# One 512-column product in place of two of 256 columns in 83 weight units of a float32 block kernel, the halves added by VectorE

## What is computed

```python
xn = rmsnorm(h, norm1_g)                      # h: (1, 256, 1024)
p = xn @ w_in                                 # 1024 x 5408: attention, RWKV, gates
# attention of 8 heads, an RWKV-7 time mix of 8 heads, both gated and projected
h = h + y @ w_out
xn = rmsnorm(h, norm2_g)
q = xn @ peer_wq                              # 16 query units of 128 columns
s = einsum('thpc,hpnc->thpn', q, peer_subkeys)
top_s, top_i = top_k(s, 16)                   # then top 16 of 256 pairs per head
gates = softmax(best_s)
h = h + sum_k(gelu(u[idx] . xn) * gates * v[idx])   # 16384 experts, 128 a head and token
return rmsnorm(h, normf_g)
```

## Time and profile before

| | us |
|---|---|
| median of 3 runs | 1074.61 (1073.79 to 1075.15) |
| the profiled execution, its own time | 1073.91 |
| its span, first to last instruction | 1072.1 |
| TensorE busy | 1063.4 (7680 products) |
| VectorE busy | 694.3 |
| ScalarE busy | 613.7 |
| GpSimd busy | 475.5 |
| mean DMA rate | 169 GB/s |

### The profile page before, as it was taken

The page is one execution under the profiler, slowest core; times in us unless marked ns, Lnnn a source line. Parts: engine busy times, 40 slices in busy tenths (PEclk is TensorE's granted clock), DMA queues, the critical chain, the costliest instruction groups (busy, mean ns, idle before and its releaser), DMA issues.

```text
span 1072.1 us, 23070 instructions
## 1 busy us (share of the span) xinstructions
PE 1063.4 (99%) x7680; PEld 985.2 (92%) x7680; DVE 694.3 (65%) x1475; ACT 613.7 (57%) x1122; POOL 475.5 (44%) x224
## 2 busy tenths in 40 slices
PE   9999999999999999999999999999999999999997
PEld 8999899999999999999999999998888888888886
DVE  7754862555549997065888888865555555555554
ACT  6763465556564445546777777765554444554444
POOL 4784623686148888878777777750000000000000
PEclk9999999999999999999999999999999999999999
DMA  7562302456535555555444444445555555555553
GB/s 266 170 205 98 119 20 81 137 179 225 180 129 180 190 178 176 185 177 174 155 155 156 155 157 157 157 157 195 189 192 191 193 195 196 195 189 189 193 193 137
DMA packets 52131, 181.21 MB, mean 169 GB/s; under 512 B 5811, under 2 KB 7859, under 8 KB 51964
## 3 DMA queue, kind: packets, MB, share of 16 engines
q1 hardware_dynamic: 51660, 180.13, 49.9%
q10 hardware_dynamic: 432, 0.55, 0.1%
HBM read 179.60 MB, written 1.06 MB: 169 GB/s over the span
## 4 chain that ended last, share of the span: by engine, by line
PE 88%; POOL 6%; issue 5%; DVE 1%; DMA 0%; ACT 0%; POOLq 0%; ACTq 0%; DVEq 0%
PE PS L411 15%; PE PS L412 14%; PE PS L413 14%; PE PS L819 11%; PE PS L817 11%; PE PS L818 11%; POOL lo L1229 6%; PE PS L768 1%; PE PS L769 1%; PE PS L600 1%; PE PS L608 1%; PE PS L556 1%; PE PS L587 1%; DMA xT<-in_x_t 0%; PE PS L634 0%
## 5 line engine op out<-in xcount | busy, mean ns | idle before, releaser
L1229 POOL TENSOR_TENSOR lo<-raw,hi 128x1024 fp32r<-128x1024 f32 x191 | 464.7, 2438 | 206.0 <-ACT hi L868 194.1
L868 ACT CAST hi<-raw 128x1024 fp32r<-128x1024 f32 x331 | 346.3, 1047 | 210.7 <-DMA raw<-in_v_units 170.9
L411 PE MATMUL PS<-xh,hi 128*128 128x256 f32 x1352 | 389.8, 288 | 0.4 <-issue 0.2
L412 PE MATMUL PS<-xl,hi 128*128 128x256 f32 x1352 | 382.1, 283 | 0.0
L413 PE MATMUL PS<-xh,lo 128*128 128x256 f32 x1352 | 381.9, 282 | 0.0
L1277 DVE TENSOR_TENSOR lo<-raw,hi 128x1024 fp32r<-128x1024 f32 x140 | 171.6, 1226 | 157.3 <-ACT hi L868 157.2
L411 PEld LDWEIGHTS PS<-xh,hi 128*128 128x128 f32 x1352 | 258.7, 191 | 3.4 <-issue 1.5
L412 PEld LDWEIGHTS PS<-xl,hi 128*128 128x128 f32 x1352 | 258.9, 191 | 0.1
L413 PEld LDWEIGHTS PS<-xh,lo 128*128 128x128 f32 x1352 | 258.7, 191 | 0.0
L817 PE MATMUL PS<-hi,xh 128*128 128x512 f32 x512 | 199.4, 390 | 0.4 <-issue 0.4
L819 PE MATMUL PS<-lo,xh 128*128 128x512 f32 x512 | 199.2, 389 | 0.0
(11 more groups left out here) (288 smaller groups left out, 1170.0 us busy)
## 6 DMA issues: line engine op xcount, KB each, us to landing
raw<-in_u_units SPq DMA_DIRECT2D x128, 512.0 KB, 3.3
raw<-in_v_units SPq DMA_DIRECT2D x128, 512.0 KB, 3.2
raw<-in_w_in_units SPq DMA_DIRECT2D x43, 512.0 KB, 3.3
raw<-in_w_q_units SPq DMA_DIRECT2D x16, 512.0 KB, 3.3
raw<-in_w_proj_units SPq DMA_DIRECT2D x8, 512.0 KB, 4.3
raw<-in_w_out_units SPq DMA_DIRECT2D x8, 512.0 KB, 4.3
arena<-bias_rows SPq DMA_DIRECT2D x2, 512.0 KB, 5.0
arena<-in_subkeys_t SPq DMA_DIRECT2D x1, 1024.0 KB, 6.3
```

The lines of the kernel that those rows point to most:

```text
L411: mm(ps, hi[:, s, c], mh[:, k, :], start=(k == k0), stop=False)
L412: mm(ps, hi[:, s, c], ml[:, k, :], start=False, stop=False)
L868: nc.scalar.copy(hi[:, j, :], raw[:, j, :]).then_inc(hi_made, 1)
L1229: nc.gpsimd.tensor_tensor(lo[:, w, :], raw[:, w, :], hi[:, w, :].bitcast(F32), ALU.subtract).then_inc(lo_pool, 1)
```

## The change

In 83 of the units, the 64 first expert units, 8 query units (the last two fours) and 11 in-projection units (10, 12, 14, 18 to 25), the first two products of each tile become one. The operand's high and low part now lie in one tensor (`xb`, `ob`), and `wide_product` multiplies the hi weights with both in one product of 512 columns: high operand to the left half of the bank, low operand to the right half. The lo product adds 256 columns to the left half. The two halves have to be added afterwards:

- in-projection: ScalarE copies the left half as before, VectorE adds the right half to the copy (`unit_halves`), and TensorE waits for this (`halves_in`) where it waited for the copy;
- queries: the same into `qT` (`query_halves`, `halves_q`);
- experts: ScalarE copies the right half to `coef` (`right_copy`), VectorE adds it to the left half in PSUM (`expert_halves`), ScalarE applies Gelu two units later in its list (`first_half_gelu`), before the cast that follows.

During the ranking, VectorE's additions are spread by a count: `ranked(columns)` adds `columns + 105` to a sum, and each 1950 of it let one addition through, up to unit 47. The additions of units 48 to 63 have fixed places. The memsets of `coef` move behind the first two one-hot groups, with the additions of units 55 to 63 between the first nine of them.

The diff, cut to its core:

```diff
+WIDE = [10, 12, 14] + list(range(18, 26))
...
-        xh = sb("xh", [P, KT, T], F32R)
-        xl = sb("xl", [P, KT, T], F32R)
+        xb = sb("xb", [P, 2, KT, T], F32R)
+        xh, xl = xb[:, 0], xb[:, 1]
...
-        oh = nc.alloc_sbuf_tensor_at("oh", [P, KT, T], F32R, offset=arena_at + 4 * 4096)
-        ol = nc.alloc_sbuf_tensor_at("ol", [P, KT, T], F32R, offset=arena_at + 4 * 6144)
+        ob = nc.alloc_sbuf_tensor_at("ob", [P, 2, KT, T], F32R, offset=arena_at + 4 * 4096)
+        oh, ol = ob[:, 0], ob[:, 1]
...
+            def wide_product(bank, s, both, tile_ready=None):
+
+                for k in range(KT):
+                    if tile_ready:
+                        tile_ready(k)
+                    c = slice(P * k, P * k + P)
+                    mm(PS[:, bank, :], hi[:, s, c], both[:, :, k, :], start=(k == 0), stop=False, skip_group_check=True)
+                    last = mm(PS[:, bank, 0:T], lo[:, s, c], both[:, 0, k, :], start=False, stop=(k == KT - 1),
+                              skip_group_check=True)
+                return last
...
+            pe.sem_inc(halves_q, 2)
...
+                if before and before[-1] in WIDE:
+                    pe.wait_ge(halves_in, WIDE.index(before[-1]) + 1)
+                elif before and before[-1] in MIX_AT:
                     pe.wait_ge(mix_made, MIX_AT.index(before[-1]) + 1)
                 elif before:
                     pe.wait_ge(act_evac, copied(before[-1]))
                 if g == GATE_AT[0]:
                     pe.wait_ge(mid_made, 1)
-                if g < PLAIN_UNITS:
+                if g in WIDE:
+                    wide_product(unit_bank(g), g % 4, xb).then_inc(unit_done, 1)
...
-            pe.wait_ge(act_evac, copied(25))
+            pe.wait_ge(halves_in, len(WIDE))
...
+                if wide:
+                    pe.wait_ge(halves_q, 4 * i + (j + 1 - 2 * HEADS // 2))
+                    wide_product(j % 2, (U_Q + j) % 4, ob).then_inc(unit_done, 1)
+                else:
+                    product(PS[:, j % 2, 0:T], (U_Q + j) % 4, oh, ol, tile_ready=tile_ready).then_inc(unit_done, 1)
...
-                    query_unit(i, j)
+                    query_unit(i, j, wide=True)
...
+                    if q >= 2:
+                        pe.wait_ge(halves_q, 2 + 4 * (q - 2) + 4)
...
+                    wide_product(U_BANKS[j], (U_U + j) % 4, xb, tile_ready=tile_ready).then_inc(unit_done, 1)
+                else:
+                    product(PS[:, U_BANKS[j], 0:T], (U_U + j) % 4, xh, xl).then_inc(unit_done, 1)
 
             def gated_unit(i, j):
                 n = 4 * i + (j - HALF)
-                expert_unit(i, j)
+                expert_unit(i, j, wide=False)
...
+            def right_copy(i, j):
+                act.wait_ge(unit_done, 4 * i + (U_U + j + 1))
+                nc.scalar.copy(coef[:, 4 * i + j, :], PS[:, U_BANKS[j], T:2 * T]).then_inc(right_u, 1)
+
+            def first_half_gelu(i, j):
+                act.wait_ge(halves_u, 4 * i + (j + 1))
+                nc.scalar.activation(area(0, P * T)[:, bass.ds(4 * T * i + T * j, T)], PS[:, U_BANKS[j % 4], 0:T],
+                                     ACT.Gelu).then_inc(act_evac, 1)
 
+            for j in range(4):
+                hi_ahead(U_U, 0, j)
+                right_copy(0, j)
+                if j >= 2:
+                    first_half_gelu(0, j - 2)
+            with act.Fori(1, PICKS_AT) as i:
                 for j in range(4):
                     hi_ahead(U_U, i, j)
-                    act.wait_ge(unit_done, 4 * i + (U_U + j + 1))
-                    nc.scalar.activation(coef[:, 4 * i + j, :], PS[:, U_BANKS[j], 0:T], ACT.Gelu).then_inc(act_evac, 1)
+                    right_copy(i, j)
+                    first_half_gelu(i, j - 2)
             hi_ahead(U_U, PICKS_AT, 0)
             act.wait_ge(shift_made, 2)
...
+                right_copy(PICKS_AT, j)
+                first_half_gelu(PICKS_AT, j - 2)
...
+                    dve.wait_ge(act_evac, copied(g))
+                    V.tensor_tensor(v, right, v, ALU.add).then_inc(halves_in, 1)
+
+            def query_halves(i, j):
+                dve.wait_ge(act_evac, 4 * i + (2 + ACT_IN + j + 1))
+                v = qT[:, 4 * i + j, :]
+                V.tensor_tensor(v, PS[:, j % 2, T:2 * T], v, ALU.add).then_inc(halves_q, 1)
+
+            def expert_halves(i, j):
+                dve.wait_ge(right_u, 4 * i + (j + 1))
+                left = PS[:, U_BANKS[j], 0:T]
+                V.tensor_tensor(left, left, coef[:, 4 * i + j, :], ALU.add).then_inc(halves_u, 1)
+
+            summed, columns_done = [0], [0]
+
+            def ranked(columns):
+
+                columns_done[0] += columns + RANK_FIXED
+                if columns_done[0] >= RANK_PER_UNIT and summed[0] < 4 * PICKS_AT:
+                    columns_done[0] -= RANK_PER_UNIT
+                    expert_halves(summed[0] // 4, summed[0] % 4)
+                    summed[0] += 1
...
             V.tensor_tensor(kh, k2, grow, ALU.mult)
+            unit_halves(12)
             mix_in(11)
             link(V.tensor_tensor(aB, kk, aB, ALU.mult))
             V.tensor_tensor(bh[0:HD], aB[0:HD], grow[0:HD], ALU.mult)
             V.tensor_tensor(turn(bh[HD:P]), turn(aB[HD:P])[..., ::-1], turn(grow[HD:P])[..., ::-1], ALU.mult)
+            unit_halves(14)
             mix_in(12)
...
                     make_lo(U_Q, i, j)
+                    if j:
+                        query_halves(i, j - 1)
+                query_halves(i, 3)
             operand_low(1, XL_POOL, KT)
...
                         link(V.tensor_tensor(picked, bpf[:, r].unsqueeze(2).to_broadcast([P, 64, TOPK]),
                                              iota_ps[:, 0:TOPK].unsqueeze(1).to_broadcast([P, 64, TOPK]), ALU.is_equal))
+                        ranked(1024)
...
+            for u in range(summed[0], 4 * PICKS_AT):
+                expert_halves(u // 4, u % 4)
             dve.wait_ge(exp_made, 1)
             b4 = bvs.rearrange("p n (h k) -> p (n h) k", k=TOPK)
             link(V.tensor_reduce(small[:, 0:16], b4, AX_X, ALU.add))
...
+                expert_halves(PICKS_AT, j)
...
             one_hots(0, 0)
+            expert_halves(PICKS_AT + 1, 2)
             one_hots(0, 1)
+            for k in range(HALF, NKEYS, 4):
+                u = 4 * (PICKS_AT + 1) + 3 + (k - HALF) // 4
+                last = V.memset(coef[:, k:k + 4, :], 1.0)
+                if u < HALF:
+                    expert_halves(u // 4, u % 4)
+            last.then_inc(coef_made, 2)
 
             dve.wait_ge(act_evac, 2 + ACT_IN + 16 + HALF)
...
+RANK_FIXED, RANK_PER_UNIT = 105, 1950
```

More of the change, by code:

```diff
@@ L472, in in_unit @@
                 before = [p for p in range(g) if unit_bank(p) == unit_bank(g) and p not in range(26, 30)]
-                if before and before[-1] in MIX_AT:
+                if before and before[-1] in WIDE:
+                    pe.wait_ge(halves_in, WIDE.index(before[-1]) + 1)
+                elif before and before[-1] in MIX_AT:
                     pe.wait_ge(mix_made, MIX_AT.index(before[-1]) + 1)
@@ L717, in _, with query_unit @@
                         tile_ready=(lambda k: pe.wait_ge(y_made, k + 1)) if k == 0 else None).then_inc(unit_done, 1)
-            def query_unit(i, j, tile_ready=None, first=False):
+            def query_unit(i, j, tile_ready=None, first=False, wide=False):
                 if first and j == 0:
@@ L1153, in _ @@
                     hi_ahead(U_U, i, j)
-                    act.wait_ge(unit_done, 4 * i + (U_U + j + 1))
-                    nc.scalar.activation(coef[:, 4 * i + j, :], PS[:, U_BANKS[j], 0:T], ACT.Gelu).then_inc(act_evac, 1)
+                    right_copy(i, j)
+                    first_half_gelu(i, j - 2)
+            for j in (4, 5):
+                first_half_gelu(HALF // 4 - 1, j - 2)
             def low_one_hots(i, j):
@@ L1307, in _, with unit_halves @@
             V.memset(rms_eps, RMS_EPS).then_inc(eps_made, 1)
+            def unit_halves(*gs):
+                for g in gs:
+                    if g < U_QKV:
+                        v = gate(GATE_AT.index(g))
+                        right = PS[:, unit_bank(g), T:2 * T]
+                    elif g < U_QKV + CT:
+                        v, right = query_reversed(qA[:, g - U_QKV, :]), PS[:, unit_bank(g), T:2 * T]
+                        right = right.rearrange("p (n t) -> p n t", t=P)
+                    else:
+                        v, right = kA[:, g - U_QKV - CT, :], PS[:, unit_bank(g), T:2 * T]
+                    dve.wait_ge(act_evac, copied(g))
[15 more added lines that the diff above has]
+                    summed[0] += 1
             def square_x(q):
@@ L1427, in _ @@
             mix_in(14)
+            unit_halves(18, 19, 20, 21)
             dve.wait_ge(rows_out, 16)
@@ L1445, in _ @@
                                 ALU.mult).then_inc(mat_sb, 1)
+                if k % 4 == 3:
+                    unit_halves(U_QKV + CT + k // 4)
             dve.wait_ge(mat_sb, 16)
```

(8 more changed lines are left out.)

19 lines of the change are left out of this document (12 added, 7 removed).

## The result

| | before | after |
|---|---|---|
| median, us | 1074.20 (4 runs, 1073.57 to 1075.15) | 1093.32 (4 runs, 1089.87 to 1095.55) |
| the profiled execution, its own time | 1073.91 | 1095.55 |
| its span | 1072.1 | 1093.4 |

The ratio is 1.0174, with a 95% interval of 1.0146 to 1.0203: 19.1 us slower by the medians. The prediction had the direction right and the size wrong: +8.1 us, and 1093.32 lies 6.3 us above its range. The four runs of the changed kernel took 1095.55, 1093.71, 1092.93 and 1089.87 us at mean granted clocks of 0.988, 0.991, 0.993 and 0.994. The profiled one is the slowest of the four. One execution of the run three, in experiment 5, took 1483.52 us at a mean granted clock of 0.656 and is left out of the numbers there.

A forecast was written before the change was run, and what follows sets the result against it. TensorE, busy 1063.4 of 1072.1 us, was taken as the bound. Pairs -8.8, holes and late units +1.9, +2.4, +0.7, +6.5, +0.6, +3.7 and clock +1.1 sum to +8.1 us: 1082.7 us, range 1073.5 to 1087.0.

The forecast's parts named there:

- the pairs: In 83 wide units, a 512-column and a 256-column product replace three of 256: 0.106 us saved a unit, -8.8 us.
- the clock: Products behind the hole at D run at 1.2 GHz for some 3.5 us: +1.1 us; a drop at E left to range.
- F: Hole before the attention scores, not forecast: additions of units 10, 14 and 18 to 25 were said to cost nothing.
- A: In-projection unit 14 waits for the addition of unit 12, which stands behind `kh` on VectorE: +1.9 us.
- B: Query unit 12 waits for its low part, which comes behind the addition of unit 11 on VectorE: +2.4 us.
- D: Expert unit 50 waits: 7.5 us of ranking behind the last addition delay the exponential and a Gelu: +6.5 us.
- E: Gates of unit 66 wait: seven memsets behind the addition of unit 63 delay the weighing: +3.7 us.
- Rival 2: The ranking does not hold back the exponential, so no wait at D: 8.2 us go, 1074.5 us; chance 0.15.
- rival 1: The lo product hides its weight load behind the wide one: 25 ns a pair makes good the holes; chance 0.10.
- rival 3: A wide product costs 240 ns, no cheaper than two, so the holes alone stay: 1091.5 us; chance 0.05.
- unit 51: Expert unit whose cast comes behind the delayed Gelu, then GpSimd's low part: 0.7 us late, before 0.1: +0.6 us.
- C: Scores: the tokens' low parts come behind the addition of query unit 15, so ScalarE's score copies start later: +0.7 us.

The follow-up runs named there:

- three: Mended kernel with each wide product made as two of 256 columns, the second of each unit also with a start flag: 1076.40 us, ratio 1.0034.
- experiment 5: Price of a pair: mended kernel with each wide product made as two narrow ones, run as three (1076.40 us) and three_b (1075.76 us).
- Experiment 2: Mended kernel with one edit undone at a time: at D 1080.45 us, at B 1075.31 us, at E 1077.89 us.
- three_b: As three, but the start flag stands on the first product of each unit alone: 1075.76 us, ratio 1.0018.
- only_b: Mended kernel with the low part of query unit 12 again behind the addition of unit 11: 1075.31 us, ratio 1.0005.
- only_f: Mended kernel with the addition of unit 25 again before the masked chains ahead of the attention scores: 1079.22 us, ratio 1.0046.
- mended: Changed kernel with the additions moved in VectorE's list at all six places and nothing else: 1071.48 us, ratio 0.9976 to the kernel before.
- only_d: Mended kernel with the count back to 1950 columns, so ranking stands behind the last addition and the exponential waits: 1080.45 us, ratio 1.0047.
- only_a: Mended kernel with the addition of in-projection unit 12 back behind `kh`: 1078.12 us, ratio 1.0032.

## Why the prediction was wrong, step by step

*Right.* The direction, and not by luck: the four forecast holes (14.2 us) less what the pairs saved (5.9) are +8.3 without the clock and F. TensorE without holes as the bound; the 7016 products; A, B, D and E as the places, each named with its waiting instruction, and as hole sizes within 1 us (1.9, 2.4, 6.5, 3.7 against 2.0, 2.7, 5.6, 3.9). Experiment 2 shows D, B and E as causes by undoing them one by one. D was forecast 0.9 us too long: the last product of unit 47 starts at 458.8 and is over at about 458.9, which is D0; the last addition could start at 459.54, behind its copy, and starts at 460.34 (0.8 late, 0.9 forecast), the ranking ends at 467.48, D0 + 8.6 where 9.3 was forecast, and unit 50 starts at D0 + 11.2 where 11.9 was. Rival 2 (no wait at D) and rival 1 (lo product without its columns) are out, the latter by 347 to 353 ns a pair; rival 3 (a wide product no cheaper than two) is out by three_b.

*The clock, the largest error.* The step was "half of some 3.5 us is lost, 1.7, of which the wait of unit 51 would have taken 0.6: +1.1", for D alone, with E left to the range and the others not considered. It took the pause at the end and the 3.7 us of slow products at the start as the scale. The trace shows drops behind four holes, two of them of 2.7 and 3.5 us, and three of the four lasted 6.83 us. Cost: 8.6, of which D has 1.7, the size that the prediction worked out for it; F and E have 2.7 each and B 1.6. So it was not the size of one drop that was wrong, but how many there would be. In the kept traces holes of 2.35 us (A) and below had no drop behind them, and each of the ten of 2.5 us and more had one, of 3.41 to 10.24 us; the two executions of only_b at 1072 us say that a hole of 2.5 us does not always bring one. The ledger is of the slowest execution: the fastest, at a mean clock of 0.994 and not 0.988, had by my estimate some 11 us at half clock and not 24.

*F, the missed place.* The step was "The additions of units 10, 14 and 18 to 25 come at least a unit before they are needed and cost nothing". It asked when TensorE needs the sum, and not what stands behind the addition on VectorE. What stood there was a chain that before ended at 116.2 and was wanted at 119; in the changed kernel it started 3.4 us later, over a microsecond of it TensorE's own lateness, and ran into GpSimd. With the clock it costs 7.7 us alone (only_f). The rows of before held the warning: the same operation at 1.2 and at 3.4 us within one chain.

*The pairs.* The step was "I take each at its own pace": 346.7 ns. The prediction had no row with the two widths in turn. That is one of two paces; the mean was 351.1, and 5.9 us were saved, not 8.8. Worked out for a product saved, the pair at 346.7 gives the 13.3 ns of the prediction and the one at 353.3 gives 6.7. The rule that it was weighed against (the Trainium skill, "TensorE: Matmul & The Clock Gate", section "Back-to-back issue gap", 2.5 ns a product) would give 1.7 us; three_b measures 4.3 to 4.8, between that and the 8.8 of the prediction.

*C and unit 51.* C did not happen: the scores took 7.06 us before and after. In its place three expert units waited 1.9 us together for GpSimd's low parts, which ran beside VectorE's ranking (three of them took 9.20 us where alone they take 7.2). The prediction had "two or three times 0.5 us" for this in its range and not in its sum. Unit 51 was late by nothing that can be seen, since unit 50 itself ran at half clock.

The changed kernel's excess over mended (21.8 us) is less than the sum of the five single ones (6.6 + 3.8 + 9.0 + 6.4 + 7.7 = 33.5). Part of that is shown: A was 2.35 us in the one trace and 4.7 in the other, only_d had a 3.4 us hole at unit 14 and only_d, only_b and only_a the drop near 175. Why that drop comes in some kernels and not in others is open.

## What to carry to other kernels

An instruction put into an engine's fixed list is cheap by its length and dear by its wait: ask of each one what stands behind it and who waits for that, not only when its own result is wanted. Count a hole of TensorE as more than itself: in the traces here each of 2.5 us or more cost another 1.5 to 3.2 us of products at half clock, so several moderate holes cost more than their sum. And where one row of a trace shows an operation at two durations, find out what runs beside the slow one before moving it by a unit: here a chain that started 3.4 us late ended 7.5 us late.

## What was not expected of the hardware

- The same 128x1024 operation of VectorE took 1.22 us alone and 3.31 to 3.42 beside GpSimd's low parts, and those 2.4 alone and up to 3.4 so. Beside the ranking's 128x2048 operations (L1721) a low part took 4.2 and 4.5 us in the changed kernel; two of the three short holes at expert units, near 357 and 428 us, come behind these.
- A product of 512 columns followed by one of 256 goes at 346.7 or 353.3 ns for dozens of microseconds, with unchanged code and in either layout; three of 256 go at 360.0 always.
- The clock fell to 0.50 for 3.41 us near 171 to 178 us in three kernels whose TensorE had no hole there, at a cost of 1.5 us; the traces of the changed and the mended kernel, with the same products there, have it at 1.00.
- A start flag on a product into one half of a bank also restarted the sums of the other half: three and three_b differ in that flag alone, and only three's results are wrong. Which product is lost is read from the order of the code; no run shows it by itself.
